# A two-layer hybrid decoder on one core: a reordered beginning, half-width first products at three joints, and attention values moved ahead in the mixer

## The reference

```python
def half_ffn(x, g_pre, g_post, w_gate, w_up, w_down):
    h = rms_norm(x, g_pre)
    f = (jax.nn.silu(h @ w_gate) * (h @ w_up)) @ w_down
    return x + 0.5 * rms_norm(f, g_post)

def decoder_layer(x, past_k, past_v, s0, buf, past_len, p):
    x = half_ffn(x, ..., p['ffn1_w_gate'], p['ffn1_w_up'], p['ffn1_w_down'])
    m, k_new, v_new, s_new, buf_new = mixer(rms_norm(x, p['mix_norm_pre']), past_k, past_v, s0, buf, past_len, p)
    x = x + rms_norm(m, p['mix_norm_post'])
    x = half_ffn(x, ..., p['ffn2_w_gate'], p['ffn2_w_up'], p['ffn2_w_down'])
    return x, k_new, v_new, s_new, buf_new
```

## Time and profile before

| | us |
|---|---|
| three runs | 1408.23, 1409.45, 1413.83 |
| median | 1409.45 |
| the profiled execution | 1408.98 |
| its span | 1407.3 |
| TensorE busy | 1391.1 |
| VectorE busy | 899.6 |
| ScalarE busy | 734.5 |

### The profile page before, as it was taken

How to read it: one execution, slowest core, us unless ns; L and a number is a source line. 1 busy time by engine, 2 the same in 40 slices (tenths; PEclk the granted TensorE clock), 3 DMA queues, 4 the chain that set the end, 5 groups by cost and what they waited for, 6 DMA issues and landing times.

```text
span 1407.3 us, 26950 instructions
## 1 busy us (share of the span) xinstructions
PE 1391.1 (99%) x10551; PEld 1321.4 (94%) x10551; DVE 899.6 (64%) x1508; ACT 734.5 (52%) x1210; POOL 182.6 (13%) x333
## 2 busy tenths in 40 slices
PE   7999999999999999999999999999999999999998
PEld 6999999988878999999999999999888799999998
DVE  5666544669995876663367665346899858756542
ACT  4544434489766554443365444346887665444441
POOL 1020000323262110000000000021433510000000
PEclk9999999999999999999999999999999999999999
DMA  9575455577799595545545555564868895555541
GB/s 247 150 210 150 141 147 153 156 203 230 210 310 265 145 255 150 150 139 152 155 127 149 151 149 144 152 175 141 252 206 242 287 255 154 151 149 149 148 139 50
DMA packets 391554, 249.41 MB, mean 177 GB/s; under 512 B 16513, under 2 KB 379638, under 8 KB 391428
## 3 DMA queue, kind: packets, MB, share of 16 engines
q1 hardware_dynamic: 375602, 204.94, 51.2%
q0 software_dynamic: 15520, 42.62, 9.7%
q10 hardware_dynamic: 306, 0.13, 0.0%
HBM read 242.10 MB, written 5.53 MB: 176 GB/s over the span
## 4 chain that ended last, share of the span: by engine, by line
PE 94%; DVE 2%; ACT 1%; DMA 1%; issue 1%; SPq 0%; POOLq 0%; POOL 0%; DVEq 0%; ACTq 0%
PE bank L596 25%; PE bank L598 24%; PE bank L597 24%; PE bank L862 3%; PE bank L973 2%; PE bank L877 2%; PE bank L632 2%; PE bank L636 2%; PE bank L633 2%; PE bank L1050 1%; DMA raw<-in_ffn_w_gate 1%; PE bank L827 1%; PE bank L954 1%; PE bank L1168 1%; PE bank L1090 1%
## 5 line engine op out<-in xcount | busy, mean ns | idle before, releaser
L1602 DVE TENSOR_TENSOR w_l<-raw,w_h 128x1024 fp32r<-128x1024 f32 (+1 forms) x332 | 395.4, 1196 | 295.4 <-ACT w_h L1224 295.1
L596 PE MATMUL bank<-hh,w_h 128*128 128x320 f32 x1632 | 512.9, 314 | 0.0
L598 PE MATMUL bank<-hh,w_l 128*128 128x320 f32 x1632 | 504.4, 309 | 0.0
L597 PE MATMUL bank<-hl,w_h 128*128 128x320 f32 x1632 | 504.3, 309 | 0.0
L1224 ACT ACTIVATE w_h<-raw 128x1024 fp32r<-128x1024 f32 (+1 forms) x332 | 332.3, 1030 | 141.4 <-DMA raw<-in_ffn_w_down 101.4
L596 PEld LDWEIGHTS bank<-hh,w_h 128*128 128x128 f32 x1632 | 306.4, 188 | 11.8 <-issue 8.6
L597 PEld LDWEIGHTS bank<-hl,w_h 128*128 128x128 f32 x1632 | 306.5, 188 | 0.6
L598 PEld LDWEIGHTS bank<-hh,w_l 128*128 128x128 f32 x1632 | 306.4, 188 | 0.0
L596 PE MATMUL bank<-guh,w_h 128*128 128x320 f32 x704 | 217.7, 309 | 0.0
L598 PE MATMUL bank<-guh,w_l 128*128 128x320 f32 x704 | 217.4, 309 | 0.0
L597 PE MATMUL bank<-gul,w_h 128*128 128x320 f32 x704 | 217.4, 309 | 0.0
(11 more groups left out here) (297 smaller groups left out, 1604.9 us busy)
## 6 DMA issues: line engine op xcount, KB each, us to landing
raw<-in_ffn_w_gate SPq DMA_DIRECT2D x88, 512.0 KB, 4.0
raw<-in_ffn_w_up SPq DMA_DIRECT2D x88, 512.0 KB, 3.9
raw<-in_ffn_w_down SPq DMA_DIRECT2D x64, 448.0 KB, 3.8
raw<-in_w_in SPq DMA_DIRECT2D x44, 512.0 KB, 4.0
raw<-in_ffn_w_down SPq DMA_DIRECT2D x32, 512.0 KB, 4.0
kpg<-in_cache_sb_k SPq DMA_DIRECT2D x112, 128.0 KB, 3.3
kpg<-in_cache_sb_k POOLq DMA_DIRECT2D x112, 128.0 KB, 2.7
raw<-in_w_out SPq DMA_DIRECT2D x16, 512.0 KB, 6.9
```

Source lines behind the costliest of these rows:

```text
L596: pe.matmul(out, w_h[:, slot, k, :], rhs_h[:, k0 + k, :], start=first, stop=False)
L597: pe.matmul(out, w_h[:, slot, k, :], rhs_l[:, k0 + k, :], start=False, stop=False)
L598: last = pe.matmul(out, w_l[:, slot, k, :], rhs_h[:, k0 + k, :], start=False, stop=end)
L1602: V(dve.tensor_tensor(w_l[:, slot, 0:n, :], raw[:, slot, 0:n, :], w_h[:, slot, 0:n, :].bitcast(F32), ALU.subtract), sm["w_lo"])
```

## The change

**The beginning.** The identity is loaded by ScalarE's queue, which then issues one parameter load only; the other eleven are issued by GpSimd, behind a wait for the first weight. TensorE multiplies zeros by zeros in bank 6, 14 times ahead of the transposes and 3, 1, 1, 1, 4 times behind tiles 3 to 7, once GpSimd has cleared a piece of `sq`. ScalarE places tiles 1, 3 and 5 of x. The parameters are transposed behind the first mean, and are waited for in the seventh unit.

```diff
         def _(pool):
-            pool.memset(wa2_all[:, :, :], 0.0).then_inc(sm["wa2_cleared"], 1)
-            pool.wait_ge(sm["wa2_cleared"], 1)
+            pool.memset(sq[:, 1, :], 0.0).then_inc(sm["first_cleared"], 1)
+            pool.memset(wa2_all[:, :, :], 0.0).then_inc(sm["first_cleared"], 1)
+            pool.wait_ge(sm["first_cleared"], 2)
+            pool.wait_ge(w_loaded[0], 16)
+            for name, at_ in PAR.items():
+                if at_:
...
+                    pool.dma_start(parn[at_:at_ + src.shape[0], :, :], src).then_inc(sm["par_loaded"], 16)
...
         def _(pe):
+            pe.wait_ge(sm["first_cleared"], 1)
+            def keep_busy(count):
+                for n in range(count):
+                    pe.matmul(bank[6][:, 0:P], sq[:, 1, 0:P], sq[:, 1, 0:P], start=True, stop=True)
+            keep_busy(14)
             pe.wait_ge(sm["ident_loaded"], 16)
...
                 if j >= 4:
-                    pe.wait_ge(sm["x_placed"], j - 3)
+                    pe.wait_ge(sm["xa_placed" if j % 2 else "x_placed"], j // 2 - 1)
...
+                if j >= 3:
+                    keep_busy((3, 1, 1, 1, 4)[j - 3])
...
         def _(act):
-            for name, at_ in PAR.items():
-                src = ...
-                act.dma_start(parn[at_:at_ + src.shape[0], :, :], src).then_inc(sm["par_loaded" if at_ else "pre_loaded"], 16)
+            act.dma_start(const[:, 0:P], ins["const"][:, 0:P]).then_inc(sm["ident_loaded"], 16)
+            act.dma_start(parn[0:8, :, :], ins["ffn1_norm_pre"].rearrange("l (r c) -> r l c", c=P)).then_inc(sm["pre_loaded"], 16)
```

```diff
+                def first_tile(c, first):
+                    for q, b_ in enumerate(banks):
+                        slot = SLOT[u0 + q]
+                        pe.wait_ge(sm["w_lo"], u0 + q + 1)
+                        pe.matmul(b_[:, c], w_h[:, slot, 0, :], hh[:, 0, c], start=first, stop=False, skip_group_check=True)
+                        pe.matmul(b_[:, c], w_l[:, slot, 0, :], hh[:, 0, c], start=False, stop=False, skip_group_check=True)
                 for k in range(KD):
+                    if k == 0 and M % 3 < 2:
+                        pe.wait_ge(sm["h_first"], M)
+                        first_tile(slice(0, T // 2), True)
                     pe.wait_ge(sm["h_hi"], 8 * M + k + 1)
...
+                            if q == 0:
+                                first_tile(slice(T // 2, T), False)
```

```diff
+                pe.wait_ge(*at("o_r", 2))
+                turn_weights(4)
                 values(3)
                 pe.wait_ge(*at("o_read", 2))
                 gla_outputs((2, 3))
-                turn_weights(4)
+                new_values(1)
+                values(4)
+                pe.wait_ge(*at("pz_w", 3))
                 outputs(0)
-                pe.wait_ge(*at("pz_w", 3))
...
                 last.then_inc(sm["conv_mean"], 1)
-                new_values(1)
-                values(4)
                 turn_weights(5)
...
                 pe.wait_ge(*at("knm_ready", 1))
+                pe.wait_ge(*at("so_done", 4))
                 state_products(0)
```

More of the change, by code:

```diff
@@ L604, in first_entry @@
                 for q, b_ in enumerate(banks):
[L605 to L612, removed]
                     slot = SLOT[q]
@@ L629, in entry @@
                         slot = SLOT[u0 + q]
+                        if k == 0 and M % 3 < 2:
+                            if q == 0:
+                                first_tile(slice(T // 2, T), False)
+                            continue
                         if k == 0:
                             pe.wait_ge(sm["w_lo"], u0 + q + 1)
-                        pe.matmul(b_[:, 0:T], w_h[:, slot, k, :], hh[:, k, :], start=(k == 0), stop=False)
-                        pe.matmul(b_[:, 0:T], w_l[:, slot, k, :], hh[:, k, :], start=False, stop=False)
+                        pe.matmul(b_[:, 0:T], w_h[:, slot, k, :], hh[:, k, :], start=(k == 0), stop=False, skip_group_check=True)
+                        pe.matmul(b_[:, 0:T], w_l[:, slot, k, :], hh[:, k, :], start=False, stop=False, skip_group_check=True)
                     pe.wait_ge(sm["h_lo"], 8 * M + k + 1)
                     for q, b_ in enumerate(banks):
-                        last = pe.matmul(b_[:, 0:T], w_h[:, SLOT[u0 + q], k, :], hl[:, k, :], start=False, stop=(k == KD - 1))
+                        last = pe.matmul(b_[:, 0:T], w_h[:, SLOT[u0 + q], k, :], hl[:, k, :], start=False, stop=(k == KD - 1), skip_group_check=True)
                         if k == KD - 1:
@@ L715, in ffn @@
                             keys_early_copied(1, 0)
+                        if M == 0 and i == t == 1:
+                            pe.wait_ge(sm["par_ready"], 1)
                         if k2 % 2 and i == t == 1:
@@ L724, in ffn @@
                             x_mean(M, bank[3])
+                            if M == 0:
+                                pe.wait_ge(sm["par_loaded"], 16 * len(PAR) - 16)
+                                for l in range(L):
+                                    last = pe.transpose(bank[2][:, l * P:l * P + NPAR], parn[:, l, :], cst_("ident", NPAR, NPAR))
+                                last.then_inc(sm["par_turned"], 1)
                             if k2 % 2:
@@ L1077, in outputs @@
                     for p_ in range(2):
-                        last = pe.transpose(bank[7][:, 256 + p_ * P:256 + (p_ + 1) * P], oq[:, p_ * P:(p_ + 1) * P], cst_("ident"))
+                        last = pe.transpose(bank[OQ_BANK[g]][:, 256 + p_ * P:256 + (p_ + 1) * P], oq[:, p_ * P:(p_ + 1) * P], cst_("ident"))
                     last.then_inc(sm["oq_turned"], 1)
@@ L1647, in post_norm @@
                     dve.wait_ge(sm["x_ready"], 9 * N + j)
+                    if more and j == 2:
+                        h_lo(N + 1, 0)
                     done = term(j)
-                    if more:
+                    if more and j > 2:
                         h_lo(N + 1, j - 2)
@@ L1678, in settle_in @@
                     for q in range(5, 8):
+                        if M == 0 and q == 6:
+                            place_parameters()
                         lo(u0 + q)
@@ L1740, in _ @@
             place_x(2)
-            place_x(3)
             h_lo(0, 0)
+            h_lo(0, 1)
             place_x(4)
-            h_lo(0, 1)
-            lo(0)
-            place_x(5)
-            h_lo(0, 2)
-            place_x(6)
-            h_lo(0, 3)
-            place_x(7)
-            for j in range(4, KD):
+            h_lo(0, 2)
+            h_lo(0, 3)
+            place_x(6)
+            h_lo(0, 4)
+            place_x(7)
+            lo(0)
+            for j in range(5, KD):
                 h_lo(0, j)
```

55 lines of the change are left out of this document (32 added, 23 removed).

## The result

Twelve runs each, in turn: 1411.3 us median (1408.07 to 1413.3) against 1409.25 (1406.67 to 1413.83) before. The ratio is 1.0016, with a 95% interval of 1.0009 to 1.0024: the change makes the kernel slower, by 1.3 to 3.4 us. Forecast was no movement (1409.2, 0.05 us under the measured median of before). The time lies in the forecast's range and within 0.5% of before, but the kernel is slower, by a little, where no loss was forecast. The profiled execution took 1412.18 us, 3.2 over that of before, with a span of 1410.5.

What follows compares the result with a forecast made beforehand. TensorE, 99% busy, was taken as the bound; -2.4 (start) - 0.7 (joints) + 4.0 (mixer hole) - 1.6 + 1.0 (clock) - 0.3 (`vpg1b`) = 0.0, so 1409.2 us median, range 1403.0 to 1415.3.

Steps and rivals of the forecast that it cites:

- The first weight: At the start: fewer competing loads let the first weight land earlier, gaining 1.7 us, at most 2.65.
- The clock at the start: At the start: products on zeros bring the fast clock by the first product, gaining 0.7 us, between 0 and 1.4.
- R3: Rival, chance 0.08: the start runs at the slow level throughout, +3.6 instead of -2.4, giving 1415.2 us.
- The joints: At joints M = 1, 3, 4: half products 0.111 us apart save 0.23 us each, -0.7 in all.
- R2: Rival, chance 0.09: at three joints a half product costs the f32 price 0.27, adding 7.6 us: 1416.8.
- -0.46 per joint: At the joints: alternative estimate from the skill's 69 ns for 160 columns, -1.4 us in all; not adopted.
- The hole: In each mixer before values(5): TensorE waits 1.9 us for ScalarE's copy into `wT`; +4.0 for both layers, turn included.
- R1: Rival, chance 0.14: the mixer hole doesn't come, so terms +4.0 and +1.0 go, leaving 1404.2 us.
- R4: Rival, chance 0.07: full start gain of 4.05 us and no mixer hole, giving 1402.5 us.
- The wait for `vpg1b`: Second layer: loads issued behind values(4) are served some 4 us earlier, removing a wait of 0.3 us.
- -1.6: Second-layer mixer near 1111: full-width products replace transposes and narrow products, so the clock fall and its 1.6 us go.
- taken +1.0: In the mixer: TensorE standing still for 1.9 us may cost new clock falls, 1.6 each; between 0 and 3.2.

Runs made afterwards that it cites:

- e2: Kernel before with only the half products at joints M = 1, 3, 4 and the earlier first `hl`: 1408.31 us, ratio 1.0003.
- e3: Kernel before with only the mixer's new order, both layers: 1414.3 us, ratio 1.0051.
- e10: Same kernel as e9 but with the beginning of the kernel before: 1407.64 us, ratio 0.999.
- e7: Changed kernel without the 24 products on zeros at the beginning: 1413.48 us, ratio 1.0035.
- e4: Changed kernel with the mixer's order of before, keeping the new beginning and joints: 1406.72 us, ratio 0.9993.
- e8: Changed kernel run once more, unchanged: 1411.43 us, ratio 1.0015.
- e1: Kernel before with the new beginning alone (identity on ScalarE's queue, late parameters, 24 products on zeros): 1407.77 us, ratio 1.0003.
- e12: The same file as e1, run again for its spread: 1408.56 us, ratio 1.0003.
- e5: Changed kernel with ScalarE's `place_weights(5)` moved directly behind `norms((2,3))`: 1405.57 us, ratio 0.9979.
- e9: Changed kernel with TensorE's `turn_weights(5)` directly behind the prompt products and ScalarE's `place_weights(5)` between the two norms: 1406.12 us, ratio 0.9981.
- e6: Changed kernel with seven unused f32 identity products inside the wait before values(5): 1408.48 us, ratio 1.0.

## Why the prediction was wrong, step by step

- **The first weight, "I take 1.7".** Mis-sized: about nothing. The profile of before had its first product at 15.41; with the same old beginning e2, e3 and e10 have it at 14.56, 14.96 and 15.34, and the new one has 14.23, 15.00, 14.79, 14.56, 15.26, 14.92 and 15.35 (and 15.30 in e7, 17.05 in e4). The 1.19 us that the two profiles show lies inside that spread. One execution's landing time was taken for the kernel's.
- **The clock at the start, "I take half, 0.7".** Mis-sized the other way: 1.58 in the profile, 2.05 as e7 less e8 (medians, so with the low stretches of either in them). Of the new beginnings with products on zeros, all but e4's had the fast level at the first product, so R3 falls. In e7, with transposes alone ahead of them, the first products stayed at the slow level until 20 us. The Trainium skill's rule on transposes ("TensorE: Matmul & The Clock Gate", Part 4: they don't count as activity for the clock) fits e7; e4's fall among the transposes fits it too, but had a wait of 1.16 us ahead of it.
- **The joints, 0.111 us a half product.** Right: from 250.65 to 252.51, 16 products at 0.111 with the first's extra 0.1, 0.25 a joint, -0.75 in all, so R2 falls. The 69 ns that the prediction worked out from the Trainium skill ("Back-to-back issue gap", same page) is its gap of an isolated product, and the section says itself that this under-counts at few columns in a stream that loads weights. Here a 160-column product with its own weights takes 0.111 us. The "-0.46 per joint" does not come out of that figure either: 16 x 0.069 behind 253.54 ends at 254.64, 0.91 before 255.55.

```profile
251.17 0.27 PE L637 MATMUL bank<-hh,w_h 128*128 128x160 f32 x1
251.28 0.28 PE L638 MATMUL bank<-hh,w_l 128*128 128x160 f32 x1
251.39 0.28 PE L637 MATMUL bank<-hh,w_h 128*128 128x160 f32 x1
```

- **The hole, 1.9 us per layer.** Right in place, cause and size (1.92 and 1.93), and so the rivals R1 and R4 fall. The 0.2 for the turn was 0.1 to 0.2.
- **"The wait for `vpg1b` ... -0.3".** 0.49. Its meaning was missed: the values' loads were a second bound of the mixer, just covered. It doesn't enter this sum, but it is why the beginning alone (e1, e12) gives nothing.
- **The clock in the mixer, "-1.6" and "taken +1.0".** This is the step that failed. The sum lets the low stretch near 1111 go because other products come into its place, and counts only the two holes as places for new ones, half of one each. The first part, the -1.6, is a wrong reading of the cause. What comes into that place is not "full-width products" but `new_values(1)` and values(4), the latter with 32 weight columns. The stretch is gone there in the changed kernel's profile, but with the same order at this place e5 and e9 have it again, directly behind the same products as before had it (e5, TensorE's timeline and the window from 1109.58 on):

```profile
1107.52 1.85 PE L1078 MATMUL bank<-qt,st 64*128 64x8 f32 x32
1109.30 0.99 PE L991 MATMUL bank<-svn,wTn 128*128 128x256 f32 x2
1110.21 3.27 PE L1001 MATMUL bank<-vpg1a,wT 128*32 128x256 f32 x32
...
1109.58:1112.99 3.41, 3.41 (x30) 1.41 (x33) 1.54 (x2) 1.24 (x3) 0.88 (x3) 0.50 1.04 347
```

  The second part left out most of the new ones. The changed kernel's profile has three, 1.55, 1.59 and 1.62: one behind a hole, two at values(2), for which there was no term. Over the four profiles of kernels with an idle hole (the changed one, e3, e7, e8) there are eight low stretches in the mixer; over the ten without (before, e1, e2, e4, e5, e6, e9 to e12) six. Of these fourteen, three begin at the end of a hole, and the other eleven all begin within a microsecond behind the GLA outputs, which end with 32 products of 8 columns (`qt`, `st`), whatever stands behind them: a turn, values(2) or `new_values(1)`.

  Those outputs stand four times in each profile. That they bring the fall is not shown, since no run changes them; that the products inside the stretch don't decide it is what before against e5 and e9 shows. So the term "-1.6" took for a property of the order what comes and goes between executions, and is tied to what the change leaves in place. All three falls behind a hole came in a layer whose values(2) had one too; why, and why values(2) is hit more often in the kernels with a hole (five of eight against three of twenty), stays open.

With -0.1 for the weight, -1.6 for the clock at the start, -0.75, +4.05 and -0.5, the sum is +1.1 to 1408.98 without its mixer's clock terms, close to the 1.2 of e8's paragraph. Some half a low stretch more than before, on average, makes up the rest of the 2 us measured. That the forecast came within 2.1 us is in part luck: the weight's 1.6 us too much and the start's clock 0.9 too little cancel in part, and the two clock terms of the mixer, -0.6 together, stand for about +0.9.

## What to carry to other kernels

When a step of a busy engine is moved ahead, follow the other engine's chain that starts behind what was pushed back, and move its copy too: one ScalarE line turned +2 us into -3. Before a start is made faster, look at which transfer lands just in time later on: a wait of 0.3 us on a DMA is the edge of a bound, and what is saved ahead of it is lost there. Take a landing time or a low clock from one profile as one draw, and keep its whole spread in the range. And before counting a low stretch as gone, look at what ran ahead of it and not only at the products in it: here a change of the latter left it standing.

## What the hardware showed

A wait of 1.9 us between narrow products was enough for the clock to fall behind it in three of the eight holes profiled (0.51 to 0.52, 3.52 instead of 1.93 us for 32 products), and with seven products of the identity in it in neither of two. The other eleven low stretches in the mixer began directly behind a run of 32 products of 8 columns each, 0.058 us apart (1.85 us for 32). 24 products on zeros at the beginning gave the fast level from the first product in all profiles with them but one. In that one (e4) the clock was 0.50 from 11 to 17 us, behind a wait of 1.16 us for x. Why ScalarE starts on the first weight anywhere between 11.3 and 13.3 us, and whether the late parameters help it at all, is open.
